# Five of sixteen PLE projection products moved into other layer norms, in place of matmuls on constants

## The reference, cut to what matters

```
h = layer_norm(ALPHA*h + 0.5*swiglu(h))            # ffn0 (layer 0), ffn2 (layer 1)
mix = conv and S5 (layer 0) or sparse attention (layer 1)
h = layer_norm(ALPHA*h + mix)                       # ab (layer 0), c (layer 1)
h = layer_norm(ALPHA*h + 0.5*swiglu(h))            # ffn1 (layer 0), ffn3 (layer 1)
h = h + (p[i] @ ple_w_proj[i]) * sigmoid(h @ ple_w_gate[i])   # PLE; p[i] is 512 x 256
```

## Time and profile before

| | us |
|---|---|
| median of 3 runs | 2883.22 |
| lowest, highest | 2882.93, 2883.66 |
| the profiled execution, its own time | 2883.02 |
| its span, first to last instruction | 2881.2 |
| PE busy | 2797.4 |
| DVE busy | 1770.6 |
| ACT busy | 623.7 |
| POOL busy | 315.0 |

### The profile page before, as it was taken

How to read it: one execution, slowest core, us unless ns; L and a number is a source line. 1 busy time by engine, 2 the same in 40 slices (tenths; PEclk the granted TensorE clock), 3 DMA queues, 4 the chain that set the end, 5 groups by cost and what they waited for, 6 DMA issues and landing times.

```text
span 2881.2 us, 34220 instructions
## 1 busy us (share of the span) xinstructions
PE 2797.4 (97%) x13390; PEld 2145.7 (74%) x13390; DVE 1770.6 (61%) x3753; ACT 623.7 (22%) x1360; POOL 315.0 (11%) x301
## 2 busy tenths in 40 slices
PE   9999999999999999999999899999999999999985
PEld 6888886668888877888864587888877766885321
DVE  4788688785766475566358766677356445664223
ACT  1322121022221022221022412222022464001001
POOL 0000020020000100000101430000201373001221
PEclk9999999999999999999999999999999999999998
DMA  4223433121322222132211111232222201257998
GB/s 170 117 103 124 131 122 121 48 77 78 117 88 103 88 88 88 60 117 103 102 62 59 44 59 66 88 117 91 100 74 95 103 16 59 88 223 286 424 424 329
DMA packets 62885, 349.51 MB, mean 121 GB/s; under 512 B 8174, under 2 KB 14446, under 8 KB 23936
## 3 DMA queue, kind: packets, MB, share of 16 engines
q1 hardware_dynamic: 45792, 320.88, 29.1%
q10 hardware_dynamic: 12064, 17.98, 1.8%
q0 software_dynamic: 4864, 8.40, 0.8%
HBM read 337.79 MB, written 14.16 MB: 122 GB/s over the span
## 4 chain that ended last, share of the span: by engine, by line
PE 89%; DVE 4%; DMA 3%; SPq 2%; ACT 1%; issue 1%; POOL 0%; ACTq 0%; DVEq 0%; POOLq 0%
PE bank L927 33%; PE bank L1125 31%; PE bank L538 6%; PE bank L547 5%; SPq L3882 2%; PE bank L3944 2%; DMA ring<-in_weights 2%; PE bank L2785 2%; PE bank L576 2%; PE bank L3370 2%; PE bank L2769 1%; PE bank L3963 1%; PE bank L568 1%; PE bank L3007 0%; PE bank L672 0%
## 5 line engine op out<-in xcount | busy, mean ns | idle before, releaser
L927 PE MATMUL bank<-area,mixed 128*128 128x256 f32 x2264 | 508.4, 379 | 2.4 <-DVE mixed L949 1.8
L927 PEld LDWEIGHTS bank<-area,mixed 128*128 128x128 f32 x2264 | 429.6, 190 | 62.2 <-DVE mixed L949 2.5
L927 PE MATMUL bank<-area,ring 128*128 128x256 f32 x1536 | 346.3, 379 | 0.1
L1125 PE MATMUL bank<-area 128*128 128x256 f32 x1440 | 323.9, 379 | 0.0
L927 PEld LDWEIGHTS bank<-area,ring 128*128 128x128 f32 x1536 | 291.4, 190 | 40.3 <-DVE area L968 0.5
L1125 PEld LDWEIGHTS bank<-area 128*128 128x128 f32 x1440 | 273.6, 190 | 37.2
L1125 PE MATMUL bank<-buf_b,area 128*128 128x256 f32 x1040 | 239.3, 379 | 0.0
L1125 PE MATMUL bank<-buf_a,area 128*128 128x256 f32 x1040 | 239.1, 379 | 0.0
L1125 PEld LDWEIGHTS bank<-buf_b,area 128*128 128x128 f32 x1040 | 197.5, 190 | 27.1 <-issue 0.3
L1125 PEld LDWEIGHTS bank<-buf_a,area 128*128 128x128 f32 x1040 | 197.6, 190 | 26.9
L949 DVE TENSOR_TENSOR mixed<-ring 128x512 f32<-128x512 f32 (+2 forms) x95 | 65.0, 684 | 223.1 <-PE bank L927 222.8
(11 more groups left out here) (641 smaller groups left out, 4355.6 us busy)
## 6 DMA issues: line engine op xcount, KB each, us to landing
ring<-in_weights SPq DMA_DIRECT2D x236, 1024.0 KB, 4.8
area<-in_weights SPq DMA_DIRECT2D x35, 1024.0 KB, 27.8
buf_b<-in_weights SPq DMA_DIRECT2D x10, 1024.0 KB, 26.5
buf_a<-in_weights SPq DMA_DIRECT2D x8, 1024.0 KB, 25.1
const<-in_weights SPq DMA_DIRECT2D x5, 1024.0 KB, 27.7
norm<-in_weights SPq DMA_DIRECT2D x4, 1024.0 KB, 23.0
mixed<-in_weights SPq DMA_DIRECT2D x4, 1024.0 KB, 27.2
area<-area ACTq DMA_DIRECT2D x20, 128.0 KB, 2.4
```

Source lines behind the costliest of these rows:

```text
L927: mm = pe.e.matmul(b, w[:, k * P:(k + 1) * P], x(INPUT_OF[p], unit.lo + k), start=(unit.key, BANK_OF[p]) not in begun, stop=unit.last and ...
L1125: mm = pe.e.matmul(out[:, half * H:(half + 1) * H], weights[:, at:at + P], x(name, d), start=fresh and half == 0 and d == 0, stop=half == ...
```

## The change

Of each layer's eight projection products, some are made in earlier norms, where the products on constants stood: products 0 and 1 of layer 0 in norm ab (one before the spread of the scales, one behind it), products 0 and 1 of layer 1 in norm ffn2 in the same way, and product 2 of layer 1 in norm c, behind the scales only. Their results wait in three places (`early_proj`). In ffn1 six products are left and in ffn3 five, of which one is made before the spread of the scales and the others behind it. Their weight pieces move in the packed order to the new places of use: four pieces of layer 0 ahead of ffn1's lead, four of layer 1 behind ffn2's down weights, two of layer 1 ahead of ffn3's lead. p has a new place on chip that the wide sums overwrite, so it is loaded four times, by ACT: in the ab stage and at the end of the wide groups of ffn1, ffn2 and ffn3; DVE waits for the last product that reads p before it writes wide sums.

```diff
@@ weight_plan
     plan["ab_out"] = thin_pieces("ab_w_out", (0,), HALVES)
+    plan["ple0_early"] = dense("ple_w_proj", (0,), PLE, 0, 2 * P)
     plan["ffn1_lead"], plan["ffn1_wide"] = lead_pieces(0, 1), wide_pieces(0, 1)
     plan["ffn1_down"] = ffn_pieces(0, 1)
-    plan["ple0_proj"] = dense("ple_w_proj", (0,), PLE, 0, D)
+    plan["ple0_proj"] = dense("ple_w_proj", (0,), PLE, 2 * P, D - 2 * P)
...
     plan["ffn2_down"] = ffn_pieces(1, 0)
+    plan["ple1_early"] = dense("ple_w_proj", (1,), PLE, 0, 2 * P)
...
     plan["c_out"] = thin_pieces("c_w_out", (0,), NEXT)
+    plan["ple1_third"] = dense("ple_w_proj", (1,), PLE, 2 * P, P)
     plan["ffn3_lead"], plan["ffn3_wide"] = lead_pieces(1, 1), wide_pieces(1, 1)
     plan["ffn3_down"] = ffn_pieces(1, 1)
-    plan["ple1_proj"] = dense("ple_w_proj", (1,), PLE, 0, D)
+    plan["ple1_proj"] = dense("ple_w_proj", (1,), PLE, 3 * P, D - 3 * P)
@@ plan_mean
+    SPREAD_TO = {"ab": (0, 0, 1), "ffn2": (1, 0, 1), "c": (1, None, 2)}
+    BEFORE_SCALES = 1
+
-    def plan_mean(st, beside=None):
+    def plan_mean(st, beside=()):
...
-        if beside is None:
+        if st in SPREAD_TO:
+            layer, first, second = SPREAD_TO[st]
+            if first is not None:
+                plan_ple_proj(layer, first, order[0])
+            plan_scales(st)
+            plan_ple_proj(layer, second, order[1])
+            return
+        if not beside:
             plan_scales(st)
             return
-        others = itertools.cycle(order[4:] + order[:2])
-        for m in range(KD):
-            if m == KD // 2:
+        for n, ((layer, m), b) in enumerate(zip(beside, order[4:] + order[:2])):
+            if n == BEFORE_SCALES:
                 plan_scales(st, order[3])
-            beside(m, next(others))
-        g.turn = next(others)
+            plan_ple_proj(layer, m, b)
+        g.turn = order[4]
@@ tensor_stats and tensor_scales, the same in both
-        if st not in BESIDE:
+        if beside:
+            beside()
+        else:
             idle_products(pe, ("squares", st), (square_read, STATS[st] + 1), IDLE_ROOT)
@@ scalar_wide_ffn, behind the last wide product
         if i == 0:
             scalar_s5_load(ac)
+        else:
+            scalar_load_p(ac, (i - 1) // 2 + (i == 2))
@@ vector_wide_up
+    P_READ_BY = {1: ("proj", 0, 1), 2: ("proj", 0, KD - 1), 3: ("proj", 1, 2)}
...
         vector_wide_inputs(ve, i, h, r, ready)
+        if i in P_READ_BY:
+            ve.wait_ge(*g.done(P_READ_BY[i]))
@@ the places
-    pt, proj = chunks(region(81 * H, 2 * T), 2), chunks(region(BASE + 2 * T, KD * T), KD)
+    pt, proj = chunks(region(86 * H, 2 * T), 2), chunks(region(BASE + 2 * T, KD * T), KD)
+    early_proj = region(81 * H, T), region(83 * H, T), stat[:, :]
...
+    P_LOADS = {"ple0_early": 1, "ple0_proj": 2, "ple1_early": 3, "ple1_third": 3, "ple1_proj": 4}
+    N_EARLY = 2, 3
...
     def tensor_ple_proj(pe, stream, layer, ms):
-        pe.wait_ge(p_loaded, 16 * (layer + 1))
         for m in ms:
-            product(pe, stream, g, ("proj", layer, m), plan[f"ple{layer}_proj"][m], cols(pt))
+            name, n = proj_weights(layer, m)
+            pe.wait_ge(p_loaded, 16 * P_LOADS[name])
+            product(pe, stream, g, ("proj", layer, m), plan[name][n], cols(pt))
@@ the ab stage, ACT
+        ac.wait_ge(*g.done(("y", KC - 1)))
+        scalar_load_p(ac, 0)
         ac.wait_ge(z_done, KC)
@@ tensor_program (layer 1 likewise; norm c has a product behind the scales only)
-        tensor_stats(pe, "ab", buf_b, ab_ready)
-        tensor_scales(pe, "ab")
+        tensor_stats(pe, "ab", buf_b, ab_ready, projections(0, 0, 1))
+        tensor_scales(pe, "ab", projections(0, 1, 2))
         tensor_wide_ffn(pe, s, 1, buf_a, buf_b, ln_ready("ab"))
-        tensor_stats(pe, "ffn1", buf_b, ffn_ready(1))
-        tensor_ple_proj(pe, s, 0, range(0, 4))
-        tensor_scales(pe, "ffn1")
-        tensor_ple_proj(pe, s, 0, range(4, KD))
+        tensor_stats(pe, "ffn1", buf_b, ffn_ready(1), projections(0, N_EARLY[0], N_EARLY[0] + BEFORE_SCALES))
+        tensor_scales(pe, "ffn1", projections(0, N_EARLY[0] + BEFORE_SCALES, KD))
@@ scalar_program (layer 1 likewise)
         scalar_sqrt(ac, "ab")
+        scalar_ple_proj(ac, 0, (0,))
         scalar_ln(ac, "ab", buf_b, buf_a, KD)
-        scalar_wide_ffn(ac, 1, "ffn1", buf_a, buf_b, lambda e: scalar_load_p(e, 0))
+        scalar_ple_proj(ac, 0, (1,))
+        scalar_wide_ffn(ac, 1, "ffn1", buf_a, buf_b)
         scalar_sqrt(ac, "ffn1")
-        scalar_ple_proj(ac, 0, range(KD // 2))
-        scalar_ln(ac, "ffn1", buf_b, buf_a, 2 * KD, lambda e, n: scalar_ple_proj(e, 0, (KD // 2 + n,)))
+        scalar_ple_proj(ac, 0, (N_EARLY[0],))
+        scalar_ln(ac, "ffn1", buf_b, buf_a, 2 * KD, lambda e, n: scalar_ple_proj(e, 0, (N_EARLY[0] + 1 + n,)))
+        scalar_ple_proj(ac, 0, range(N_EARLY[0] + 1 + KD // 2, KD))
```

More of the change, by code:

```diff
@@ L584, in bank @@
         return banks[(groups or g).bank[label]]
-    BESIDE, IDLE_ROOT, IDLE_SCALE, IDLE_RMS = ("ffn1", "ffn3"), 6, 6, 3
+    IDLE_ROOT, IDLE_SCALE, IDLE_RMS = 6, 6, 3
     IDLE_RANK, IDLE_SLOTS, IDLE_ROWS = 10, 8, 5
@@ L680, in idle_products, with tensor_stats @@
             pe.e.matmul(bank(label)[:, 0:P], C("ident"), C("mean"), start=True, stop=True)
-    def tensor_stats(pe, st, r, ready):
+    def tensor_stats(pe, st, r, ready, beside=None):
         i = NORMS.index(st)
@@ L700, in tensor_stats, with tensor_scales @@
         spread(pe, ("means", st), mean_c)
-        if st not in BESIDE:
+        if beside:
+            beside()
+        else:
             idle_products(pe, ("squares", st), (square_read, STATS[st] + 1), IDLE_ROOT)
-    def tensor_scales(pe, st):
+    def tensor_scales(pe, st, beside=None):
         pe.wait_ge(inverted, STATS[st] + 1)
         spread(pe, ("scales", st), scale_c)
-        if st not in BESIDE:
+        if beside:
+            beside()
+        else:
             idle_products(pe, ("squares", st), (square_read, STATS[st] + 1), IDLE_RMS if st in RMS else IDLE_SCALE)
@@ L1974, in vector_thin_residual, with proj_weights, projected @@
         vector_mix(ve, following, ("S4",))
-    pt, proj = chunks(region(81 * H, 2 * T), 2), chunks(region(BASE + 2 * T, KD * T), KD)
+    pt, proj = chunks(region(86 * H, 2 * T), 2), chunks(region(BASE + 2 * T, KD * T), KD)
+    early_proj = region(81 * H, T), region(83 * H, T), stat[:, :]
+    PROJ_PLAN = ((("ple0_early", 2), ("ple0_proj", 6)), (("ple1_early", 2), ("ple1_third", 1), ("ple1_proj", 5)))
+    P_LOADS = {"ple0_early": 1, "ple0_proj": 2, "ple1_early": 3, "ple1_third": 3, "ple1_proj": 4}
+    N_EARLY = 2, 3
+    def proj_weights(layer, m):
+        for name, n in PROJ_PLAN[layer]:
+            if m < n:
+                return name, m
+            m -= n
+    def projected(layer, m):
+        return early_proj[m] if m < N_EARLY[layer] else proj[:, m, :]
     gates = [region((10 + 2 * i) * T, 2 * T) for i in range(2)]
@@ L1992, in plan_ple_proj @@
     def plan_ple_proj(layer, m, bank):
-        g.add(("proj", layer, m), (proj_done, KD * layer + m + 1), blocks=B(f"ple{layer}_proj", m), bank=bank)
+        g.add(("proj", layer, m), (proj_done, KD * layer + m + 1), blocks=B(*proj_weights(layer, m)), bank=bank)
     def tensor_ple_proj(pe, stream, layer, ms):
-        pe.wait_ge(p_loaded, 16 * (layer + 1))
         for m in ms:
-            product(pe, stream, g, ("proj", layer, m), plan[f"ple{layer}_proj"][m], cols(pt))
+            name, n = proj_weights(layer, m)
+            pe.wait_ge(p_loaded, 16 * P_LOADS[name])
+            product(pe, stream, g, ("proj", layer, m), plan[name][n], cols(pt))
     def scalar_ple_proj(ac, layer, ms):
@@ L2002, in scalar_ple_proj @@
             ac.wait_ge(*g.done(("proj", layer, m)))
-            ac.e.activation(proj[:, m, :], bank(("proj", layer, m)), ACT.Copy).then_inc(proj_done, 1)
+            ac.e.activation(projected(layer, m), bank(("proj", layer, m)), ACT.Copy).then_inc(proj_done, 1)
     def plan_ple(layer):
@@ L2040, in gated @@
             ve.wait_ge(proj_done, KD * layer + m + 1)
-            ve.step(tt(gate_of(m), gate_of(m), proj[:, m, :], ALU.mult))
+            ve.step(tt(gate_of(m), gate_of(m), projected(layer, m), ALU.mult))
             ve.settle()
@@ L3851, in build_in @@
     COMMON = IN_RING[:1] + EARLY + MERGE + IN_RING[RING - 1:] + IN_RING[1:RING - 1] + [(norm[:, :], pos_loaded, 1)]
-    HOMES = COMMON + [(flat_a[:, 0:BLOCK], p_loaded, 2), (flat_a[:, BLOCK:2 * BLOCK], turn_loaded[0], PPC // 2), (flat_mixed, comb_stored, 0)]
+    HOMES = COMMON + [(flat_a[:, 0:BLOCK], p_loaded, 4), (flat_a[:, BLOCK:2 * BLOCK], turn_loaded[0], PPC // 2), (flat_mixed, comb_stored, 0)]
     def home(block, homes):
@@ L4226, in build_in @@
     plan_wide_ffn(1)
-    plan_mean("ffn1", lambda m, b: plan_ple_proj(0, m, b))
+    plan_mean("ffn1", [(0, m) for m in range(N_EARLY[0], KD)])
     plan_ple(0)
@@ L4233, in build_in @@
     plan_wide_ffn(3)
```

(31 more changed lines are left out.)

## The result

The changed kernel takes 2888.83 us (median of 13 runs, 2887.02 to 2891.38) against 2883.23 for the one before, timed beside it (13 runs, 2882.28 to 2885.99). The ratio is 1.0019, 95% interval 1.0012 to 1.0027: slower by 5.6 us, between 3.5 and 7.8. That lies just inside the bound of 0.2%. The forecast was +3.3, and the time lies in the range given.

What follows compares the result with a forecast made beforehand. The prediction took PE as the bound: what counts is when it can start its next work. Its terms, -7.5 + 8.1 + 2.8 = +3.4 us, gave 2886.5 us, with a range of 2881.5 to 2891.0.

Steps and rivals of the forecast that it cites:

- Step 1: Norms ffn1 and ffn3: fewer projection products let the gate start earlier, gaining 3.2 and 4.3 us, 7.5 in all.
- the bank's wait: Gate of ffn3: its fourth bank, emptied by an ACT copy, comes late and the gate waits about 0.7 us.
- Steps 2 and 3: Five products into ab, ffn2 and c cost nothing, at most 0.2 us each; loading p four times costs nothing.
- Step 4: Leads of ffn1 and ffn3: seven blocks for six slots delay sum 0; two waits of 4.06 us, 8.1 in all.
- Step 5: Behind those two waits: the clock falls once at each place, at 1.4 us each, 2.8 in all.
- its own range: The forecast's range for the run time, 2882.6 (waits 3.9, no fall) to 2888.9 us, at chance 0.68.
- The slower one: Rival: two clock falls at each wait, 3.4 us per place, 2890.5 in all; chance 0.22 together with a shrunken gain.
- The faster one: Rival: first lead block's slot freed early, so the quarter is in time and no wait is paid; 2875.6 us, chance 0.08.
- The gain that is not taken: Rival: something else than PE holds the gate, 7.5 shrinks to about 4, end 2890; chance 0.22 together with two falls.

Runs made afterwards that it cites:

- run 5: Kernel before, with only products 0 and 1 of layer 1 moved into norm ffn2 and one of ffn3's six ahead of the scales; 2880.45 us, ratio 0.9988.
- run 1: Changed kernel, with the first lead block's slot freed when PE has read the block's last piece; 2876.33 us against 2883.91, ratio 0.9975.
- run 3: Kernel before, with empty columns ahead of the leads of ffn1 and ffn3 in the packed weights, nothing else moved; 2897.42 us, ratio 1.0050.
- run 2: Changed kernel, with sixteen products on constants between products 0 and 1 of the first wide group of ffn1 and ffn3; 2884.42 us, ratio 1.0001.
- run 4: Kernel before, with empty columns ahead of both leads, and p loaded behind the wide groups of ffn1 and ffn3; 2896.45 us, ratio 1.0043.
- run 7: The changed kernel again, unedited, on another chip; 2888.5 us, ratio 1.0018.
- run 6: Changed kernel, with the early slot release and ACT's copies in ffn3 behind chunks 1, 3, 5, 7 instead of 2, 4, 6, 8; 2875.99 us, ratio 0.9975.

## Why the prediction was right, and which term was off

The sign, the mechanism and the places held; one term was too small. The waits stand here as the prediction counts them, from start to start: 4.05 + 3.99, and 1.95 - 0.17 behind each.

| step | forecast | trace of the changed kernel |
|---|---|---|
| 1, ffn1 | -3.2 | -3.2 |
| 1, ffn3, after the bank's wait | -4.3 | -4.1 |
| 2 and 3, products in other norms, p loads | 0 | under 0.2 in all |
| 4, two waits (start of product 1) | +8.1 | +8.0 |
| 5, the clock behind them, with all else lost there | +2.8 | +3.6 |
| sum | +3.4 | +4.3 |
| spans / medians | | +5.5 / +5.6 |

**Step 1** held to 0.2. The fill could be read off as the reciprocal's end plus 1.00 plus so many products of 1.72; the products show again in run 5, where ffn3 has five behind the scales: 2129.05 - 2120.47 = 8.58. The bank that is late next came where it was named, at 0.9 in place of 0.7.

**Steps 2 and 3** held. In ab the scales come 0.06 behind the reciprocal and the lead 2.94 behind the scales, against 3.06 before. Run 1 has all of these products and loads and still takes the whole gain of step 1 (-7.6 between the medians, -7.3 by the trace), so nothing is hidden there.

**Step 4** held and is shown from three sides: run 3 makes the wait without the products, run 1 the products without the wait, run 5 two products without the block. It was at most 0.1 too long at each place; the first load landed 4.70 and 4.65 after its issue, not 4.8.

**Step 5, "the fall, once at each place, at 1.4", is the mis-sized term.** The falls came, once at each place, but the cut of a part "as the slow stretch may lie in the gap itself" was wrong here: the 1.7 fell on the dense work behind the wait, and 0.1 more goes at each place without any fall. So the two places cost 3.6, not 2.8. Run 2 separates these. The price also varies. Eight waits of 3.8 to 6.1 us were left unfilled in four profiles (the changed kernel twice, runs 3 and 4): seven were followed by a fall, with 1.95 to 3.2 lost behind them, and one by none. The Trainium skill's rule that speaks against the change ("TensorE: Matmul & The Clock Gate", section "HAM oscillation — how this bites in real kernels": a kernel that waits for a DMA between bursts is throttled again at each wait) is borne out at those seven, and not at the eighth, of 3.91.

One sum does not come out: the lower end of its own range, 2882.6, was to hold waits of 3.9 and no fall, but 2883.2 - 7.5 + 7.8 is 2883.5. The forecast does not hang on it.

**The rivals.** The slower one, two falls at each wait, happened at one place in one profile (run 7) and in run 3, where the waits were longer; never at both waits of the changed kernel in one profile. The faster one did not happen in the change, but its mechanism is real: run 1 is exactly it, forecast 7.5 under before (2875.6) and measured 7.6 under (2876.33). The gain that is not taken did not happen.

**What stays open.** Of the 5.6, 4.3 lies at the places of the change. That the whole came to 5.6 and not to 4.3 is nothing that the prediction foresaw. The other 1.2 of the profile is a net of differences at places that the change leaves alone, falls of the clock above all, some of which one profile has and another has not. The fall behind the 2.77 gap is such a one. It came in the changed kernel both times and in runs 3, 4, 5 and 6 (in run 4 the gap was 2.94), and not in the one profile of before nor in runs 1 and 2. The stretch behind it in run 1 and in run 3:

```profile
2180.00:2184.00 4.00, 4.00 (x13) 2.20 (x12) 0.00 (x0) 0.55 (x1) 0.00 (x0) 1.00 0.00 0
...
2200.00:2204.00 4.00, 4.00 (x10) 2.04 (x10) 0.75 (x2) 2.99 (x4) 0.00 (x0) 0.76 0.06 23
```

Run 1 has all the moved products and no fall; run 3 has none of them and a fall. So this fall does not go with the products, and what decides it stays open. The interval of the result (3.5 to 7.8) holds 4.3 as well.

## What to carry to other kernels

Where weights are prefetched through a fixed number of slots, count the blocks that are alive at once around every piece that is moved: four pieces (a quarter of a block) ahead of one stage and two ahead of another made seven blocks for six slots at each, and the two waits of about 4 us cost more than moving five products gained. Two products whose weights fitted into room that was there kept their gain (run 5). Look then at what frees the slot: giving it back at the last read of the block, not at the end of the whole product, cost nothing and took the loss away. A PE gap of about 4 us between dense stretches should be priced with a fall of the clock, which here came at seven of eight and cost 1.7 on top of 3.9 where it came once; if the wait itself cannot go, products on constants in it save that part.

## What the runs showed of the hardware that was not expected

- The landing of the same three ring loads behind the same p load was 5.34 at one place and 7.00 at the other of one profile (run 3). Without a p load beside them it was 4.64 to 4.78 at all six places in the changed kernel (twice) and run 4. Runs 3 and 4 differ in that load alone: 5.34 against 4.76 in ffn1, 7.00 against 4.64 in ffn3, so it costs 0.6 and 2.4, in one profile each. Why so unequal stays open.
- The clock can stay down for two stretches behind one wait: the loss was 3.0 by the windows behind a wait of 3.95 (run 7), and 1.7 behind another of the same length in the same profile.
- One wait of 3.91 had no fall (run 4), while the gap near 2190, 2.77 long in eight of nine profiles and 2.94 in the ninth, had a fall in six of them and none in three. The length of the gap alone does not decide it.
